# Key scores of a product-key expert layer: ranked on VectorE in the background instead of being stored and read back

## The reference, cut to what matters

```python
q = (xb @ w_query).reshape(PEER_BLOCK, PEER_HEADS, 2, half)
s1 = jnp.einsum('thd,kd->thk', q[:, :, 0], sub_keys[0])   # 128 scores a half
s2 = jnp.einsum('thd,kd->thk', q[:, :, 1], sub_keys[1])
v1, i1 = lax.top_k(s1, 16)
v2, i2 = lax.top_k(s2, 16)
cand = v1[..., :, None] + v2[..., None, :]                # 256 sums
cidx = i1[..., :, None] * 128 + i2[..., None, :]
top_s, top_pos = lax.top_k(cand, 16)
eidx = take_along_axis(cidx, top_pos)
gate = softmax(top_s)
act = einsum('td,thkd->thk', xb, expert_u[eidx])
out = einsum('thk,thkd->td', gate * gelu(act), expert_v[eidx])
```

## Time and profile before

| | us |
|---|---|
| median of 3 runs (4188.24 to 4190.41) | 4189.36 |
| the profiled execution | 4191.42 |
| its span in the profile | 4189.6 |
| VectorE busy | 2891.2 |
| TensorE busy | 3272.4 |
| GpSimd busy | 2246.9 |
| ScalarE busy | 642.9 |

### The profile page before, as it was taken

The page is one execution under the profiler, slowest core; times in us unless marked ns, Lnnn a source line. Parts: engine busy times, 40 slices in busy tenths (PEclk is TensorE's granted clock), DMA queues, the critical chain, the costliest instruction groups (busy, mean ns, idle before and its releaser), DMA issues. The chain is left out here.

```text
span 4189.6 us, 33991 instructions
## 1 busy us (share of the span) xinstructions
PE 3272.4 (78%) x9782; PEld 1758.9 (42%) x9798; DVE 2891.2 (69%) x6507; ACT 642.9 (15%) x1771; POOL 2246.9 (54%) x2277
## 2 busy tenths in 40 slices
PE   6977898788888988787888888887778666655666
PEld 1444575654444544455444445444445222222222
DVE  2212111588787777988878877887788878788885
ACT  0020000221012212122110122120212011101010
POOL 0001000366664556556666545765676777776775
PEclk9968898899998899889999888998889888888888
DMA  7316444799997999999999978999999999999998
GB/s 257 123 34 168 104 121 141 278 406 404 393 388 268 330 381 397 347 390 375 397 402 390 384 278 319 391 389 390 383 406 400 409 409 405 409 409 401 399 409 332
DMA packets 578895, 1405.12 MB, mean 335 GB/s; under 512 B 44731, under 2 KB 276347, under 8 KB 578683
## 3 DMA queue, kind: packets, MB, share of 16 engines
q0 software_dynamic: 320080, 1165.57, 71.6%
q1 hardware_dynamic: 223070, 196.45, 15.1%
q10 hardware_dynamic: 35560, 40.91, 2.8%
HBM read 1369.31 MB, written 33.44 MB: 335 GB/s over the span
## 5 line engine op out<-in xcount | busy, mean ns | idle before, releaser
L1786 PE MATMUL peer_psA<-peer_vring,peer_diag 128*128 128x512 f32 x2464 | 1383.9, 702 | 621.2 <-DMA peer_vring<-in_expert_v,peer_idx 477.4
L2435 DVE CUSTOM_DVE_ANT_0 peer_uring<-peer_uring,peer_psH 128x1024 f32<-128x1024 f32 x1088 | 1319.3, 1213 | 356.9 <-DMA peer_uring<-in_expert_u,peer_idx 352.4
L1510 POOL DMA_INDIRECT peer_vring<-in_expert_v,peer_idx x1088 | 1108.3, 1019 | 796.3 <-PE peer_psA L1786 504.5
L1500 POOL DMA_INDIRECT peer_uring<-in_expert_u,peer_idx x1088 | 1096.7, 1008 | 706.6 <-DVE peer_idx L2411 374.9
L1786 PEld LDWEIGHTS peer_psA<-peer_vring,peer_diag 128*128 128x128 f32 x2464 | 509.4, 220 | 1339.8 <-issue 1155.9
L2451 DVE SCALAR_TENSOR_TENSOR peer_acc<-peer_vring,peer_coef,peer_acc 128x1024 f32<-128x1024 f32 x463 | 595.1, 1285 | 82.5 <-DMA peer_vring<-in_expert_v,peer_idx 75.7
L1755 PE MATMUL peer_psB<-peer_w,keep_hT 128*128 128x256 f32 x1152 | 274.1, 394 | 18.8 <-DMA peer_w<-in_w_query 17.7
L1681 PE MATMUL peer_psB<-keep_hT,peer_w 128*128 128x384 f32 (+1 forms) x864 | 277.5, 480 | 4.7 <-DMA peer_w<-in_w_in 4.7
L1699 PE MATMUL peer_psB<-keep_hT,peer_w 128*128 128x384 f32 (+1 forms) x768 | 252.6, 484 | 22.5 <-DMA peer_w<-in_w_attn_o 22.5
L1755 PEld LDWEIGHTS peer_psB<-peer_w,keep_hT 128*128 128x128 f32 x1152 | 228.5, 200 | 76.8 <-issue 27.6
L2148 ACT ACTIVATE peer_g<-peer_g 128x16 f32<-128x16 f32 (+1 forms) x72 | 15.5, 215 | 1446.0 <-DVE peer_g L2465 1446.0
(11 more groups left out here) (244 smaller groups left out, 2904.4 us busy)
## 6 DMA issues: line engine op xcount, KB each, us to landing
peer_w<-in_w_in SPq DMA_DIRECT2D x102, 512.0 KB, 21.4
peer_w<-in_w_query SPq DMA_DIRECT2D x24, 1024.0 KB, 17.1
peer_w<-in_w_in SPq DMA_DIRECT2D x12, 1536.0 KB, 18.2
peer_uring<-in_expert_u,peer_idx POOLq DMA_INDIRECT x1088, 14.2
peer_vring<-in_expert_v,peer_idx POOLq DMA_INDIRECT x1088, 14.1
front_ring<-in_w_ada POOLq DMA_DIRECT2D x7, 2048.0 KB, 8.7
front_ring<-in_w_ada SPq DMA_DIRECT2D x5, 2048.0 KB, 8.0
peer_w<-in_w_conv_o SPq DMA_DIRECT2D x24, 384.0 KB, 21.0
```

The source lines that it names most:

```text
L1500: pool.indirect_dma_start(out=uring[:, r % U, :], out_offset=None, in_=io["expert_u"], in_offset=bass.IndirectOffsetOnAxis(ap=idx[:, s % 4 ...
L1510: pool.indirect_dma_start(out=vring[:, r % V, :], out_offset=None, in_=io["expert_v"], in_offset=bass.IndirectOffsetOnAxis(ap=idx[:, s % 4 ...
L1786: last = pe.matmul(psA[:, c * 512:(c + 1) * 512], diag[:, a % DG, :], vring[:, r % V, c * 512:(c + 1) * 512], start=first, stop=False, ski ...
L2435: dve.tensor_tensor_reduce(uring[:, r % U, :], uring[:, r % U, :], psH[:], 1.0, 0.0, ALU.mult, ALU.add, act_[:, k:k + 1]).then_inc(u_used, 1)
```

## The change

The scores don't go to DRAM. VectorE ranks each item in its background, right after ACT's copy, in place in `sc_out` (`rank`), and keeps the 16 values and indices of each half in tables `v12`, `i12` of 24 items (`RANKS = SEG * HEADS`; they had one). `experts(j)` starts from the table: 11 steps instead of 15, five of them in job s (`RANKED = 5`). ACT's copy into a slot of `sc_out` waits for the ranking of the item two before (semaphore `ranked`) where it waited for the store. `norm_shift` stands among the rankings, after items 5, 10 and 15 of a segment, at the same places of the order. VectorE's last stop in the background of a job is at 0.9. `qn` and `qT` lie in the memory of `mT`; `sc` and the DRAM tensor are gone.

```diff
-        v12, i12 = n.sb("v12", [P, 2, TOPK]), n.sb("i12", [P, 2, TOPK], U32)
+        v12, i12 = n.sb("v12", [P, RANKS, 2, TOPK]), n.sb("i12", [P, RANKS, 2, TOPK], U32)
...
-                            act.wait_ge(sc_stored[it % 2], 16 * (it // 2))
+                            act.wait_ge(ranked, it - 1)
                         act.activation(sc_out[:, it % 2, :], bank(key)[:, 0:K2], ACT.Copy).then_inc(out_of(key), 1)
-                        wait_emptied(act, key)
-                        h, j = divmod(i - 2, SEG)
-                        act.dma_start(io["scores"][(SEG * g + j) * HEADS + h],
-                                      sc_out[:, it % 2, :]).then_inc(sc_stored[it % 2], 16)
-
-            def load_scores(j):
-                it = item_of(j)
-                act.wait_ge(sc_stored[it % 2], 16 * (it // 2 + 1))
-                if j >= 2:
-                    act.wait_ge(named, j - 1)
-                act.dma_start(sc[:, j % 2, :], io["scores"][j]).then_inc(sc_in[j % 2], 16)
...
                     yield from shift_tile(g, SEG - 1)
+                    for i in range(SEG * HEADS):
+                        yield from rank(g * SEG * HEADS + i)
+                        if g + 1 < SEGS_N and i in (5, 10, 15):
+                            yield from norm_shift(g + 1, i // 5 - 1)
+
+            def rank(it):
+                a, top, at = sc_out[:, it % 2, :], v12[:, it % RANKS], i12[:, it % RANKS]
+                half = [a[:, i * KEYS:(i + 1) * KEYS] for i in range(2)]
+                yield number["score", it]
+                assert it < RANKS or chosen.index(it - RANKS) >= 0
+                wait_emptied(dve, ("score", it))
+                link.wait()
+                for i in range(2):
+                    link(dve.max(top[:, i, 0:8], half[i]))
+                link.wait()
+                for i in range(2):
+                    link(dve.max_index(at[:, i, 0:8], top[:, i, 0:8], half[i]))
+                link.wait()
+                for i in range(2):
+                    link(dve.match_replace(half[i], top[:, i, 0:8], half[i], LOW))
+                link.wait()
+                for i in range(2):
+                    link(dve.max(top[:, i, 8:16], half[i]))
+                link.wait()
+                link(dve.max_index(at[:, 0, 8:16], top[:, 0, 8:16], half[0]))
+                dve.max_index(at[:, 1, 8:16], top[:, 1, 8:16], half[1]).then_inc(ranked, 1)
...
             def experts(j):
-                t, h = divmod(j, HEADS)
-                sj = sc[:, j % 2, :]
...
-                dve.wait_ge(sc_in[j % 2], 16 * (j // 2 + 1))
-                yield from halves(lambda i, a, b: link(dve.max(v12[:, i, 0:8], a)))
...
-                yield from halves(second)
-                yield from halves(lambda i, a, b: link(dve.max(v12[:, i, 8:16], b)))
-                yield from halves(lambda i, a, b: link(dve.max_index(i12[:, i, 8:16], v12[:, i, 8:16], b)))
+                it = item_of(j)
+                top, at = v12[:, it % RANKS], i12[:, it % RANKS]
+                dve.wait_ge(ranked, it + 1)
+                link.wait()
...
-            RANKED, NAMED_AT = 9, 5
+            RANKED, NAMED_AT = 5, 5
...
-                    pace.up_to(limit(s, k / TOPK))
+                    pace.up_to(limit(s, min(0.9, k / TOPK)))
```

More of the change, by code:

```diff
@@ L1184, in peer @@
         DG = 12
+        RANKS = SEG * HEADS
         M = SEG * P
@@ L1226, in peer @@
         ss, rt, rs = (norm_small[:, i:i + 1] for i in range(3))
-        qn, qT, sc_out = n.sb("qn", [P, 2, K2]), n.sb("qT", [P, 2, K2]), n.sb("sc_out", [P, 2, K2])
+        sc_out = n.sb("sc_out", [P, 2, K2])
+        qn, qT = (flat[:, 2 * i * K2:2 * (i + 1) * K2].rearrange("p (s m) -> p s m", s=2) for i in range(2))
         uring, vring = n.sb("uring", [P, U, D]), n.sb("vring", [P, V, D])
-        h2, sc = n.sb("h2", [P, D]), n.sb("sc", [P, 2, K2])
+        h2 = n.sb("h2", [P, D])
         diag = n.sb("diag", [P, DG, P])
@@ L1260, in peer @@
             n.sem("x1_stored"), n.sem("h_stored"), n.sem("tail_kept"), n.sem("tail_stored"))
-        sc_stored, sc_in, h2_in = n.sems("sc_stored", 2), n.sems("sc_loaded", 2), n.sem("h2_loaded")
+        ranked, h2_in = n.sem("ranked"), n.sem("h2_loaded")
         best_neg, gate_exp, gate_used = n.sem("best_neg"), n.sem("gate_exp"), n.sem("gate_used")
@@ L2118, in _ @@
             load_h2(0)
-            load_scores(0)
-            load_scores(1)
             load_x1(0)
@@ L2125, in _ @@
                 t, h = divmod(s, HEADS)
-                if s + 2 < JOBS:
-                    load_scores(s + 2)
                 if h == 0 and 0 < t < NT:
@@ L2155, in _ @@
         def _(dve):
-            link = Link(dve, own)
+            link, chosen = Link(dve, own), []
             def background():
@@ L2161, in background @@
                     if g:
-                        for i in range(SEG):
-                            yield from norm_shift(g, i)
                         for z in range(4 * SEG):
@@ L2351, in experts @@
             def experts(j):
-                t, h = divmod(j, HEADS)
-                sj = sc[:, j % 2, :]
[L2355 to L2359, removed]
-                dve.wait_ge(sc_in[j % 2], 16 * (j // 2 + 1))
-                yield from halves(lambda i, a, b: link(dve.max(v12[:, i, 0:8], a)))
-                def second(i, a, b):
-                    link(dve.max_index(i12[:, i, 0:8], v12[:, i, 0:8], a))
-                    link(dve.match_replace(b, v12[:, i, 0:8], a, LOW))
-                yield from halves(second)
-                yield from halves(lambda i, a, b: link(dve.max(v12[:, i, 8:16], b)))
-                yield from halves(lambda i, a, b: link(dve.max_index(i12[:, i, 8:16], v12[:, i, 8:16], b)))
+                it = item_of(j)
+                top, at = v12[:, it % RANKS], i12[:, it % RANKS]
+                dve.wait_ge(ranked, it + 1)
+                link.wait()
                 c, c2 = cand.rearrange("p a b -> p (a b)"), sc2
-                link(dve.tensor_tensor(cand, v12[:, 0, :].unsqueeze(2).broadcast_to([P, TOPK, TOPK]),
-                                       v12[:, 1:2, :].broadcast_to([P, TOPK, TOPK]), ALU.add))
+                link(dve.tensor_tensor(cand, top[:, 0, :].unsqueeze(2).broadcast_to([P, TOPK, TOPK]),
+                                       top[:, 1:2, :].broadcast_to([P, TOPK, TOPK]), ALU.add))
                 yield
@@ L2398, in experts @@
                 link.wait()
-                link(dve.tensor_tensor(eq[:], eq[:], i12[:].unsqueeze(2).broadcast_to(shape), ALU.mult))
+                link(dve.tensor_tensor(eq[:], eq[:], at.unsqueeze(2).broadcast_to(shape), ALU.mult))
+                chosen.append(it)
                 yield
@@ L2545, in layer @@
     io["vd"] = nc.dram_tensor("value_rows", (PT, P, AW), F32, kind="Internal").ap()
-    io["scores"] = nc.dram_tensor("key_scores", (JOBS, P, 2 * KEYS), F32, kind="Internal").ap()
     with ExitStack() as whole:
```

## The result

The changed kernel takes 4203.66 us (median of 7 runs, 4196.32 to 4212.10) against 4189.36 us: slower, a ratio of 1.0035 with a 95% interval of 1.0023 to 1.0047. The forecast was 4165. The profiled execution has a span of 4204.9 us against 4189.6, and the rest of this part says where the 15.3 us come from.

What follows compares the result with a forecast made beforehand. DMA engines bound nearly everywhere, VectorE second. -16 (a), +1 (b, c), +19 (d), -8 (e), -14 and -6 (f) give -24 us: 4165 us against 4189.36; 8-in-10 range 4128 to 4206.

Steps and rivals of the forecast that it cites:

- (a): Score transfers removed, 0.36 us each where the DMA engines are the bound: 44 loads in jobs without rankings, -16 us.
- (b): Lead before job 0: the first job's indices are ready sooner, so the first gather comes 5.3 us earlier.
- (c): Jobs 0 to 2: VectorE +12.8 us later, less 12 us of ring cover; gathers end +1 us, lead included.
- (d): Jobs 21 to 26: 24 rankings for 6, +31 us left after waits, less 12 of ring cover: +19 us.
- (e): Jobs 45 to 51: 48.5 us more ranking fits into 51.4 us of VectorE's waits for rows; -8 us.
- (g): Query jobs: ScalarE's copy newly waits for the ranking two items before; taken at 0, up to +16 us.
- The cover: Rings of gathered rows in the query jobs absorb 12 us of VectorE's lag; bounds 0 and 17.
- (f): VectorE-bound jobs with one ranking less each: attention's seven jobs -14 us, jobs 18 to 20 -6 us.
- Rival 1: Query jobs: rings cover nothing, V gathers wait through TensorE and ScalarE for rankings; +19, 4208 us; chance 0.18.
- Rival 2: All transfer savings come through, VectorE's waits for rows being late by choice; -63, 4126 us; chance 0.22.

Runs made afterwards that it cites:

- light: Changed kernel with fewer V rows on VectorE, the others to TensorE, where the rankings stand: 4182.55 us, ratio 0.9977 to the kernel before.
- deep: Changed kernel with five slots of sc_out instead of two, so ScalarE's copy waits for an older ranking: 4205.32 us, ratio 1.0030 to the kernel before.
- late_q: Changed kernel with no VectorE background at k = 0 to 3 of the query jobs only: 4182.44 us, ratio 0.9971 to the kernel before.
- burst20: Kernel before with twenty unused additions, 24.6 us in one piece, on VectorE in each of six tail jobs: 4256.86 us, ratio 1.0166.

## Why the prediction was wrong

**(a) The transfers: right where the DMA engines are the bound.** The forecast took 0.36 us; put back alone, a load of the tail costs 0.29, and 0.26 to 0.38 by the tails of the other variants, so 0.36 stands within what was measured. So does the figure of the Trainium skill: its "DMA: Bandwidth & Descriptors" ("Anatomy of one DMA") gives bytes over 436 GB/s, an estimated 0.30 us for 128 KB. The 44 loads are then worth 11 to 17 us, for 16.

**(b) The lead: right.** The first gather came 5.0 us earlier, for 5.3. Its time alone proves little, since the whole lead shifts from one execution to the next (the first gather of light comes at 781.69, with the same lead as the changed kernel). But from the end of the copy of the lead's last scores to the first gather it is 15.4 to 15.5 us in all five traces with the old order, and 10.1 us in the nine with the new one that rank all 128 scores: 5.3 us less, as forecast. (The first dot product was 6.2 us earlier; it too moved by up to 8 or 9 us between traces of one order.)

**(c), (d), (e) The three query stages: the failed step.** The forecast: "Then the gathers end +1 us against today", "+19 us", "-8 us", 12 in all. Measured: -6.2 + 25.5 = +19.3, +33.9 and +11.5, 64.7 in all; the jobs behind them give some of it back. Two parts are wrong.

- A wait was missing from the sum: VectorE for ScalarE's copy, 40.7 us in the trace. The prediction looked at ScalarE's new wait for the ranking (g), which deep shows to cost nothing, and not at the ranking's own wait, although the edit adds both. late_q takes it away without touching any work and gains 28.2 us in the three stages, 21 us in all. In jobs 45 to 51 it is the size of the whole miss (20.6 for 19.5 us), since 41.2 us more work would have fitted into the 51.4 us of waits for rows; late_q took back 11.9 of it, and then the DMA engines were at 1.01.
- The cover. VectorE's work was sized well: 48.7 us more in jobs 21 to 26, for 51.3; 36.6 in jobs 0 to 2, for 39.9; 41.2 in jobs 45 to 51, for 48.5. But 12 us of cover were taken off twice at once, in (c) and (d). At the ends of these stages the lag stands in full: +19.3 us for the +12.8 that (c) had for VectorE alone, +33.9 for the +31 of (d). burst20 shows that cover is not a discount on VectorE's work but a loan: the gathers run ahead, and the time comes back only while VectorE catches up. Jobs 3 and 4 have next to no wait for rows before (VectorE is idle 4.7 and 5.7 us there, 3.4 and 4.7 of it before it reads a projection) and were 48.6 and 48.2 us long after, for 49.0 and 50.0. Beyond the price of the loads, jobs 3 to 8 gave back some 4 us and jobs 27 to 33 some 6, against the 12 and 12 assumed; behind (e) the tail gave back some 5. Why so little in jobs 27 to 33 is not shown: in jobs 21 to 24 GpSimd also waits for indices, and TensorE for the diagonals, so that fewer gathers can run ahead. GpSimd's waits in jobs 21 to 26, after:

```profile
POOL peer_vring L1512 <- PE peer_psA L1788: 32.1, 5, 16.2
POOL peer_uring L1502 <- DVE peer_idx L2408: 29.8, 3, 12.5
...
POOL peer_uring L1502 <- DVE peer_act L2432: 16.5, 16, 6.1
```

Only the last of the three is the U ring being full. The first two were there before as well, with 28.8 and 19.8 us; the last had 5.2. That these waits are what limits the loan is argued, not tested.

**(f) One ranking less elsewhere: jobs 18 to 20 right, attention half.** Jobs 18 to 20 came 6.5 us shorter (2.7, 3.0, 0.8) for 6. Attention came 8.4 shorter for 14, all but 1.5 in jobs 9 to 11; the same jobs moved by up to 9 us between variants that do not touch them, so no term can be read from one trace.

**The rivals.** Rival 1 had the nearest time (4208) and the wrong mechanism: not ScalarE's wait and the banks, as deep shows (its sign, GpSimd's waits for `psA` doubled, did not come either: 35.6, 32.1 and 27.9 us in the three stages, for 23.3, 28.8 and 25.9), but VectorE's work with no cover, plus the wait that no case had. Its condition, that all rankings above the waits for rows are lost, is what happened in the stages. That its total is so near is luck in part: the three stages cost 64.7 us where it had 41, and all other jobs gained 49 where it had 22. Rival 2 is refuted by the shares of 0.90 and 0.87. The range had room for the result (it ends at 4206); the direction was wrong.

## What to carry to other kernels

When work moves from many jobs into few, add it up against the engine's own idle time in those few; a ring in front of it lets the engine fall behind for one burst, and the time comes back only with slack in the jobs just behind. For a step that is made "as soon as its input is there", look up what its producer does at that very moment: here three engines begin a job together, and a stop four steps later was worth 21 us in the query jobs, while in attention and output projection it cost 46. Bytes saved are worth nothing where another engine has become the bound.

## What the runs showed of the hardware

Six pauses of 12.3 us in VectorE's work cost nothing measurable while the DMA engines were the bound, and six of 24.6 us cost 11.1 us each. Putting back 18.9 MB in 144 transfers cost 7 to 12 us in all, some 0.05 to 0.08 us a transfer, where one in the tail cost 0.29; 50 of them fell in jobs 0 to 2 and 21 to 26, which they made no longer, and why the other 94 cost so little in sum is open.

A top-8 pass of VectorE has a fixed part that outweighs the columns of a short row: finding the indices (FIND_INDEX8) takes 0.285 us over 128 columns and 0.169 us over 16, so some 1.0 ns a column and 0.15 us besides, and its load of match values 0.07 to 0.09. The whole ranking of an item is 1.1 us shorter with 16 columns, not 7/8 shorter.

After 17.46 us without work TensorE made its first four matmuls at a granted 0.50 of its clock, 3.78 us for 1.88. GpSimd issues gathers one after the other at 1.24 us each in the tail of the kernel before (0.94 busy, 0.30 between two), close to the 1.32 us that a job of 42.3 us leaves for each of its 32, so it is nearly a bound there itself.
